# Conditioning in column groups, norm 1 by columns, attention among the gv and u chunks, and late dots that read PSUM

## The chip, the cores and the metric

One core of a Trainium2 chip runs the whole step as one program. The metric is the time of the program on the device in microseconds (us), lower is better. TensorE (PE) multiplies matrices; VectorE (DVE), ScalarE (ACT) and GpSimd (POOL) work on rows and tiles; SyncE (SP) issues most plain transfers. SBUF is the memory on the core, PSUM the eight banks (128 partitions of 512 f32 each) into which PE writes. All data is f32.

## The reference

One decoder layer for 512 prompt rows and 64 sample rows (8 sequences of 8, each with 256 cached keys), D = 1024. Cut to what matters:

```
mod = (silu(c) @ w_ada + b_ada)          # 1024 -> 6 x 1024, 9 conditions (1 prompt, 8 sample)
shift1, scale1, gate1, shift2, scale2, gate2 = mod
h = rmsnorm(x, g1) * (1 + scale1) + shift1
q, k, v, u, gv, gate_a, gate_b = split(h @ w_in)       # 7 x 1024 columns
gv = layernorm(gelu(gv), g_v, b_v); u = gelu(u)
out_b = stick_breaking_attention(q, k, v)              # 8 heads x 128
out_a = u * (causal 128x128 mix of gv rows)
x = x + gate1 * ((sigmoid(gate_a) * (out_a @ w_ba) + sigmoid(gate_b) * (out_b @ w_bb)) @ w_out)
h = rmsnorm(x, g2) * (1 + scale2) + shift2
for each of 8 heads: score 128 x 128 key pairs, keep the best 16 experts, softmax -> gates
x = x + gate2 * sum over the 128 experts of  gate * gelu(h . down[e]) * up[e]
y = rmsnorm(x, g_final)
```

Stick-breaking attention weights a key with exp(log sigmoid(z) + the sum of log sigmoid(-z) over the keys after it). Each of the 576 rows gathers 128 rows of `down` and 128 of `up`, 4 KB each, by its own expert numbers.

## The kernel before

**Tiles and groups.** The rows form five tiles of 128: prompt tiles 0 to 3 and SAMPLE, whose 64 rows stand twice in its tile. `GROUPS` is [[0], [1, 2], [3, SAMPLE]]. For each group a front runs: norm 1, q, k, v, attention, gv and u, the mix, the merge, the output projection, norm 2, the queries and the key scores. Then come the expert rows of its tiles, in the order 0, 1, 2, SAMPLE, 3.

**Events.** The expert work is written out by hand as events e = -16 ... 576, sixteen to a step of one head (two for SAMPLE), 36 steps. At event e POOL gathers `down` row e + 32 (L734, into a slot of `gather_ring` or another of eight late slots) and `up` row e + 16 (L749) with indirect DMAs in one fixed order; DVE makes the dot of a `down` row with `h2(t)` for 128 tokens at once (`dot`, L1665); ACT makes its gelu; and the `up` row is added, by `PE_SHARE` either on PE as a product with a diagonal of coefficients into banks 6 and 7 (`sum_row`, L1078) or on DVE (L1696). Every engine has its own copy of the event loop. A POOL gather waits until its slot has been used.

**Fronts.** Group 0's front runs ahead of all events on every engine. The fronts of groups 1 and 2 are generators cut into pieces, and `DUE`, from a cost list in `pieces`, says at which event each piece is taken up: group 1 from event -16 on, its first key scores asked for at event 90, its end at 126; group 2 from 128, asked at 346, its end at 380.

**Conditioning.** At the start SP loads the nine conditions, the first four chunks of `w_ada`, b_ada, both norm gains and the small constants, then x of all tiles, then the other 20 chunks. A chunk is 1024 rows x 256 columns, 1.05 MB, and there are four buffers (`NW`). ACT's Silu waits for five transfers. PE makes each chunk's nine rows with eight matmuls (L819), DVE adds b_ada to 256 columns of nine partitions, then makes (1 + scale) * gain. SP stores the result to DRAM twice (`mod_prompt`, and `mod_sample` with each row repeated eight times), waits, and only then goes on to q's chunks and to the row tables A1 = (1 + scale1) * g1 and B1 = shift1, which are read back broadcast over 128 partitions into the two buffers `row_tables`. Norm 1 on DVE multiplies x by 1/rms and A1 and adds B1; PE turns it in 128x128 blocks, and ACT copies the blocks into `hT`.

**Projections.** Weight chunks of 1024 x 256 go through the four buffers. `token_major` (L784, eight 128x256 matmuls) fills one PSUM bank per tile with 128 tokens x 256 columns, `channel_major` (L793) fills two banks with 128 channels each. Fills rotate over banks 0 to 3 with the semaphores `s_full` and `s_free`; transposes use banks 4 and 5. ACT copies q, k, v out and makes the gelu of gv and u (L1207, L1213); DVE and ACT empty the merge.

**Attention.** It goes by stages: in stage w PE makes the scores of the heads w + 1, the exponents (suffix sums) of the heads w and the outputs of the heads w - 1, two heads per stage in groups 0 and 1, one in group 2. ACT makes the log parts (abs, two relus, exp, ln: the table load of L1190 among them), then the Exp of the exponents, then copies the outputs. All stages of a group come first, then four gv chunks, then four u chunks, with the layer norm of gv on DVE beside the u chunks.

**Choices.** `choose` (DVE, top 16 keys of two halves, 256 pairs, top 16 again) is a generator of six parts, one to an event; `exponentials` on ACT and `weigh` on DVE give the gates. The choice of step m starts at event 16 (m - 2), that is a step before POOL needs its expert numbers.

Of the kernel before, what the change touches and what calls it, by code (L numbers as in the profile page):

```python
# [15 lines left out]
P = 128  # L16
# [19 lines left out]
WIDTH = 2 * P  # L36

# [13 lines left out]
CHOICES_OF = [[c for c, (m_, _, _) in enumerate(CHOICES) if m_ == m] for m in range(M)]  # L51

# [46 lines left out]

def pieces(g):  # L100

    T, heads = len(GROUPS[g]), head_groups(g)
    chunk = 7 if T == 2 else 6
    out = [("norm1", 6)] + [("project", chunk)] * 12
    out += [("attend", (8, 10, 7)[g])] * (len(heads) + 2)
    out += [("project", chunk)] * 8
# [7 lines left out]
def head_groups(g):  # L114

    items = [(i, t, hd) for i, t in enumerate(GROUPS[g]) if t != SAMPLE for hd in range(NH)]
    first = NH * sum(t != SAMPLE for ts in GROUPS[:g] for t in ts)
    items = [(first + w, *item) for w, item in enumerate(items)]
    size = 1 if g == LASTG else 2
    return [items[w:w + size] for w in range(0, len(items), size)]  # L120
# [24 lines left out]
def fill_base(g, phase):  # L145

    t = len(GROUPS[g])
    return NADA + group_base(g, 64, 16) + {"q": 0, "k": 8, "v": 8 + 4 * t, "gv": 8 + 8 * t, "u": 8 + 12 * t,
                                           "merge": 16 + 12 * t, "out": 48 + 12 * t, "query": 48 + 16 * t}[phase]
# [9 lines left out]
NCH = 48  # L159
# [3 lines left out]
def chunk_base(g, phase):  # L163

    pages = 2 * NDEC if g == LASTG else 0
    return NADA + NCH * g + {"q": 0, "k": 4, "v": 8, "gv": 12, "u": 16, "keys": 20, "values": 20 + NDEC,
                             "merge": 20 + pages, "out": 36 + pages, "query": 40 + pages}[phase]


def last_fill(n):  # L170

    if n < NADA:
        return n
    g = min((n - NADA) // NCH, LASTG)
    t = len(GROUPS[g])
    for phase, fills in (("query", 2), ("out", t), ("merge", 2), ("u", 2), ("gv", t), ("v", t), ("k", t), ("q", 2)):
        c = n - chunk_base(g, phase)
        if c >= 0:
            return fill_base(g, phase) + fills * (c + 1) - 1


def tables(g):

    kinds = ["p", "s"] if SAMPLE in GROUPS[g] else ["p"]
    return ([(w, k) for k in kinds for w in ("A1", "B1")] + [("gv", ""), ("bv", "")]
# [31 lines left out]

def build(nc, x_prompt, x_sample, cache_k, cache_v, page_table, c_prompt, c_sample, w_ada, b_ada,
# [1577 lines left out]
```

## Time and profile before

| | |
|---|---|
| time, median of 3 runs | 2562.68 us (2562.38 to 2566.64) |
| time of the profiled execution | 2551.76 us |
| span of the profiled execution | 2549.6 us, 24823 instructions |
| TensorE's mean granted clock | 0.874 of full speed |
| DMA | 849.21 MB, mean 333 GB/s; 604.05 MB of it gathers |

The profile is one execution. Its span runs from the first to the last instruction; its time and the median of the timed runs are a little larger. The page gives busy time by engine, then 40 slices of the span, then what each queue moved, the chain of work that ended last, and the costliest groups of instructions. A busy PE includes matmuls that run at a lower granted clock, and POOL's spans are rough.

### The profile page before, as it was taken

What the parts mean: (1) busy time and instruction counts of PE and PEld (TensorE: products, weight loads), DVE (VectorE), ACT (ScalarE), POOL (GpSimd) and SP (SyncE); (2) the same over time, 40 slices, a digit from 0 to 9 for tenths busy, and PEclk for the clock granted to TensorE, in tenths of its full rate; (3) what the DMA queues carried; (4) which work ended last, traced back from release to release, by engine and by line L of the source; (5) the groups of instructions that cost most, each with busy time, mean ns of one, the idle gap of its engine ahead of it and who ended that gap; (6) DMA issues with size and microseconds to landing.
All of it is one profiled execution on the core that took longest, in us unless ns stands there. A gap on an engine that the chain in (4) does not pass through costs nothing.

```text
span 2549.6 us, 24823 instructions
## 1 busy us (share of the span) xinstructions
PE 1925.6 (76%) x7928; PEld 1327.9 (52%) x7928; DVE 1565.4 (61%) x3434; ACT 535.6 (21%) x1168; POOL 1328.2 (52%) x1169
## 2 busy tenths in 40 slices
PE   6837986966899567588887789878676567667677
PEld 2336986855788444465565557656464222222222
DVE  0100115573987876776687867775779986667552
ACT  0004112164211112114522221111021112122121
POOL 0000002553555466565557656555467677777774
PEclk9968998988999788799997776888898799899999
DMA  8654787994899899899799979999999999999997
GB/s 273 202 174 151 274 281 253 344 349 168 336 379 413 338 394 373 303 412 359 263 375 405 409 282 402 377 367 367 347 370 330 347 361 369 357 382 388 371 381 297
DMA packets 218292, 849.21 MB, mean 333 GB/s; under 512 B 26383, under 2 KB 33807, under 8 KB 196586
## 3 DMA queue, kind: packets, MB, share of 16 engines
q0 software_dynamic: 165888, 604.05, 62.6%
q1 hardware_dynamic: 40148, 222.61, 23.6%
q10 hardware_dynamic: 12128, 20.98, 2.3%
q8 instruction: 64, 1.05, 0.2%
q14 instruction: 64, 0.52, 0.1%
HBM read 830.48 MB, written 16.80 MB: 332 GB/s over the span
## 4 chain that ended last, share of the span: by engine, by line
PE 39%; DMA 17%; POOL 12%; DVE 12%; issue 8%; ACT 6%; DVEq 3%; SPq 1%; ACTq 0%; POOLq 0%
PE bank L793 11%; PE bank L1078 9%; PE bank L784 9%; DMA gather_ring<-in_expert_down,expert_numbers 6%; DMA gather_ring<-in_expert_up,expert_numbers 5%; POOL gather_ring L749 5%; POOL gather_ring L734 5%; PE bank L819 3%; DVE expert_sums L1696 3%; DVE gather_ring L1665 2%; DMA v_tokens<-in_expert_up,expert_numbers 2%; POOL weight_chunks L734 2%; POOL v_tokens L749 1%; PE bank L1002 1%; DMA mod_sample<-gather_ring 1%
## 5 line engine op out<-in xcount | busy, mean ns | idle before, releaser
L734 POOL DMA_INDIRECT gather_ring<-in_expert_down,expert_numbers x488 | 584.8, 1198 | 876.5 <-DVEq L1632 400.1
L1078 PE MATMUL bank<-gather_ring,coef_diagonals 128*128 128x512 f32 x952 | 556.5, 729 | 317.9 <-ACT coef_diagonals L1323 168.0
L1665 DVE CUSTOM_DVE_ANT_0 gather_ring<-gather_ring,h_tiles 128x1024 f32<-128x1024 f32 x488 | 596.5, 1226 | 289.9 <-DMA gather_ring<-in_expert_down,expert_numbers 266.0
L749 POOL DMA_INDIRECT gather_ring<-in_expert_up,expert_numbers x510 | 569.0, 1116 | 271.7 <-issue 130.6
L1078 PEld LDWEIGHTS bank<-gather_ring,coef_diagonals 128*128 128x128 f32 x952 | 202.2, 227 | 607.2 <-issue 390.0
L793 PE MATMUL bank<-hT,weight_chunks 128*128 128x128 f32 (+2 forms) x2304 | 403.5, 336 | 7.0 <-issue 4.5
L793 PEld LDWEIGHTS bank<-hT,weight_chunks 128*128 128x128 f32 x2304 | 377.2, 199 | 51.8 <-issue 26.7
L1696 DVE SCALAR_TENSOR_TENSOR expert_sums<-gather_ring,expert_coefs,expert_sums 128x1024 f32<-128x1024 f32 x269 | 345.6, 1285 | 8.7 <-issue 8.7
L784 PE MATMUL bank<-weight_chunks,hT 128*128 128x256 f32 x960 | 211.7, 380 | 1.4 <-ACT qT L1207 1.4
L784 PEld LDWEIGHTS bank<-weight_chunks,hT 128*128 128x128 f32 x960 | 182.1, 191 | 31.5 <-issue 5.8
L1078 PE MATMUL bank<-v_tokens,coef_diagonals 128*128 128x512 f32 x264 | 130.5, 622 | 49.0 <-DMA v_tokens<-in_expert_up,expert_numbers 29.9
L1323 ACT ACTIVATE coef_diagonals<-identity,expert_coefs 128x128 f32<-128x128 f32 x304 | 108.1, 393 | 277.8 <-DVE expert_coefs L1676 117.4
L1665 DVE CUSTOM_DVE_ANT_0 weight_chunks<-weight_chunks,h_tiles 128x1024 f32<-128x1024 f32 x88 | 107.8, 1228 | 70.7 <-DMA weight_chunks<-in_expert_down,expert_numbers 67.6
L1078 PEld LDWEIGHTS bank<-v_tokens,coef_diagonals 128*128 128x128 f32 x264 | 46.6, 192 | 130.0 <-issue 87.6
L734 POOL DMA_INDIRECT weight_chunks<-in_expert_down,expert_numbers x88 | 95.1, 1081 | 26.8 <-issue 26.8
L819 PE MATMUL bank<-weight_chunks,condT 128*9 128x256 f32 x384 | 87.8, 393 | 3.0 <-DMA weight_chunks<-in_w_ada 2.7
L749 POOL DMA_INDIRECT v_tokens<-in_expert_up,expert_numbers x66 | 75.1, 1138 | 21.5 <-issue 14.0
L1379 ACT ACTIVATE expert_acts<-expert_dots 128x16 f32<-128x16 f32 x36 | 7.8, 216 | 372.3 <-DVEq L1668 372.2
L801 PE MATMUL bank<-identity,v_tokens 128*128 128x128 f32 x40 | 9.8, 427 | 86.0 <-DVE v_tokens L1465 71.6
L784 PE MATMUL bank<-weight_chunks,u_and_gv 128*128 128x256 f32 x320 | 70.5, 380 | 3.8 <-DVE u_and_gv L1532 3.7
L1430 DVE TENSOR_TENSOR gather_ring<-bank,gather_ring 9x256 f32<-9x256 f32 x24 | 9.9, 412 | 97.0 <-PE bank L819 97.0
L784 PEld LDWEIGHTS bank<-weight_chunks,u_and_gv 128*128 128x128 f32 x320 | 60.6, 190 | 15.1 <-issue 7.2
(217 smaller groups left out, 2112.1 us busy)
## 6 DMA issues: line engine op xcount, KB each, us to landing
weight_chunks<-in_w_in SPq DMA_DIRECT2D x84, 1024.0 KB
weight_chunks<-in_w_ada SPq DMA_DIRECT2D x24, 1024.0 KB
weight_chunks<-in_w_query SPq DMA_DIRECT2D x24, 1024.0 KB
weight_chunks<-in_w_branch_a SPq DMA_DIRECT2D x12, 1024.0 KB
weight_chunks<-in_w_branch_b SPq DMA_DIRECT2D x12, 1024.0 KB
weight_chunks<-in_w_out SPq DMA_DIRECT2D x12, 1024.0 KB
weight_chunks<-in_cache_k SPq DMA_DIRECT2D x16, 512.0 KB
weight_chunks<-in_cache_v SPq DMA_DIRECT2D x16, 512.0 KB
```

The costliest lines, as they stand in the source:

```text
L734: pool.indirect_dma_start(out=d_row(slot), out_offset=None, in_=down, in_offset=bass.IndirectOffsetOnAxis(ap=expert[:, t, h * TOPK + k:h * ...
L749: pool.indirect_dma_start(out=u_row(slot), out_offset=None, in_=up, in_offset=bass.IndirectOffsetOnAxis(ap=expert[:, t, h * TOPK + k:h * T ...
L784: mm = nc.tensor.matmul(out[:, 0:WC], src[:, k, :], w[:, k, :], start=(k == 0), stop=(k == KC - 1))
L793: mm = nc.tensor.matmul(out[:, 0:N], w[:, k, j * P:(j + 1) * P], src[:, k, 0:N], start=(k == 0), stop=(k == KC - 1))
L801: mm = nc.tensor.transpose(out[0:b.shape[1], j * P:j * P + b.shape[0]], b, ident[0:b.shape[0], 0:b.shape[0]])
L819: mm = nc.tensor.matmul(out[0:NG, 0:WC], cT[:, k, :], w[:, k, :], start=(k == 0), stop=(k == KC - 1))
L1002: mm = nc.tensor.matmul(bank[2][:, at], page_of(n, page)[:, hd * P:(hd + 1) * P], log_s[page][:, at], start=False, stop=(page == 1))
L1078: mm = nc.tensor.matmul(bank[6 + half], diag[:, n % 8, :], u_row(slot)[:, half * 512:(half + 1) * 512], start=(u == PE_TILE[t][0]), stop=( ...
L1323: nc.scalar.activation(diag[:, n % 8, :], ident[:], ACT.Copy, scale=coef[:, m % 2, k:k + 1]).then_inc(s_diag, 1)
L1430: nc.vector.tensor_tensor(m, read(n)[0:NG, 0:WC], m, ALU.add).then_inc(s_free[n % 4], 1)
L1665: nc.vector.tensor_tensor_reduce(out=row, in0=row, in1=h2(t), scale=1.0, scalar=0.0, op0=ALU.mult, op1=ALU.add, accum_out=dots[:, m % 2, k ...
L1696: nc.vector.scalar_tensor_tensor(out=a, in0=u_row(slot), scalar=by, in1=a, op0=ALU.mult, op1=ALU.add).then_inc(s_dsum, 1)
```

## The change

- **Conditioning.** `w_ada` is laid out by the host as 24 chunks of one modulation's 256 input rows x 1024 columns. `condition` runs four column groups: each of 256 columns writes nine partitions at partition 32q of bank 6 or 7. Eight chunks (shift1, scale1) come first; the other sixteen are put one each behind tile 0's q, k, v and gv chunks, in SP's list `CHUNKS` and on PE. DVE adds b_ada by quarters (`modulation`) and makes the gains (`with_gain`) in `modq`, 4 x 9 partitions.
- **First loads.** b_ada, the gains and the constants are issued on ACT's queue; Silu waits for the two transfers of conditions alone; x of tile 0 is the first load after them.
- **Norm 1.** PE turns scale and shift into columns (`modT`, 16 small transposes); DVE only multiplies x by 1/rms; ACT scales and shifts each 128x128 block as it copies it out of PSUM (Identity with scale and bias). For SAMPLE DVE does that with 16 small operations. The tables A1 and B1 are gone.
- **Stores.** `mod_prompt` and `mod_sample` are written in 36 DMAs on SP, after u's loads of group 0; SP waits for them before the G1 table and the merge weights.
- **gv and u among the attention stages** (`middle`): group 0 takes a gv or u chunk after each stage of two heads, group 1 goes by one head and takes one after every second stage, group 2 keeps attention first. ACT's order in a stage is now Exp, copy, log parts. Attention's buffers move to `h2_tiles` and `sigmoids`; the layer norm (`normalised`) follows at u's pieces.
- **Banks.** Fills rotate over two banks, 0 and 1; transposes use 2 and 3; attention's scores 4 and 5, its exponents bank 2 alone and its outputs bank 3 alone.
- **Times of the choices** (`CHOOSE`): tile 1's first choice is loaded at event 110, made in one go at event 111 and weighed at 117, the next at 115 to 127; the others stay. Group 1's key scores are asked for at event 106 instead of 90, its end is 127.
- **Late dots.** From step 26 (`X_FROM`) the dots read x from PSUM: ACT copies h2 of SAMPLE into banks 0 and 1 and of tile 3 into banks 4 and 5, at event 392.
- **Group 2** loads the A2 table before its first three query chunks; before it was after four.

The diff, cut:

```diff
+def middle(g):
+    attend = [("attend", w) for w in range(-1, len(head_groups(g)) + 1)]
+    fills = [(phase, c) for phase in ("gv", "u") for c in range(4)]
+    if g == LASTG:
+        return attend + fills
+    each = (1, 2)[g]
+    out = []
+    while attend or fills:
+        out += attend[:each] + fills[:1]
+        attend, fills = attend[each:], fills[1:]
+    return out
...
+AT_ONCE = CHOICES_OF[FIRST[1]][0]
+CHOOSE[AT_ONCE] = {"load": TOPK * 6 + 14, "start": TOPK * 6 + 15, "raise": TOPK * 7 + 3, "weigh": TOPK * 7 + 5}
+CHOOSE[AT_ONCE + 1] = {"load": TOPK * 7 + 3, "start": TOPK * 7 + 7, "raise": TOPK * 7 + 13, "weigh": TOPK * 7 + 15}
...
-    size = 1 if g == LASTG else 2
+    size = 2 if g == 0 else 1
...
-    for g, start, asked, heads, end in ((1, -TOPK, 90, 2, 126), (2, 8 * TOPK, 346, 3, 380)):
+    for g, start, asked, heads, end in ((1, -TOPK, 106, 2, 127), (2, 8 * TOPK, 346, 3, 380)):
...
+def chunks():
+    out = [("ada", 0, i) for i in range(8)]
...
+            if g == 0 and i < NADA - 8:
+                out.append(("ada", 0, 8 + i))
...
-            sp.dma_start(mod_p, mod9[0:1, :]).then_inc(s_modst, 16)
-            sp.dma_start(mod_s.rearrange("(b i) n -> b i n", i=DSEQ),
-                         mod9[1:NG, :].unsqueeze(1).broadcast_to([NDEC, DSEQ, NMOD * D])).then_inc(s_modst, 16)
-            sp.wait_ge(s_modst, 32)
...
+                    sp.wait_ge(s_modv, 4 * NMOD)
+                    sp.wait_ge(s_mod, 8)
...
+                    for q in range(4):
+                        sp.dma_start(rows[:, :, q], modq[32 * q:32 * q + 1]).then_inc(s_modst, 16)
+                        for i in range(DSEQ):
+                            sp.dma_start(by_token[:, i, :, q], modq[32 * q + 1:32 * q + NG]).then_inc(s_modst, 16)
+                    sp.wait_ge(s_modst, 16 * 4 * (DSEQ + 1))
...
-                if f >= 4:
-                    pe.wait_ge(s_free[f % 4], f // 4)
-                return bank[f % 4]
+                if f >= 2:
+                    pe.wait_ge(s_free[f % 2], f // 2)
+                return bank[f % 2]
...
+            def condition(i):
+                m, part = divmod(i, 4)
+                w = weight(NUMBER["ada", 0, i]).rearrange("p k n -> p (k n)")
+                if m >= 2 and part == 0:
+                    pe.wait_ge(s_modv, 4 * (m - 1))
+                for kk in range(2):
+                    for q in range(4):
+                        at = kk * D + q * QUARTER
+                        mm = nc.tensor.matmul(bank[6 + m % 2][32 * q:32 * q + NG, 0:QUARTER], cT[:, 2 * part + kk, :],
+                                              w[:, at:at + QUARTER], start=(part == 0 and kk == 0),
+                                              stop=(part == 3 and kk == 1))
+                mm.then_inc(s_ada, 1)
...
+                for q in range(4):
+                    rows = slice(32 * q, 32 * q + NG)
+                    nc.vector.tensor_tensor(modq[rows, m, :], bank[6 + m % 2][rows, 0:QUARTER], adaq[rows, m, :],
+                                            ALU.add).then_inc(s_modv, 1)
...
+                        for j in range(4):
+                            k = 4 * half + j
+                            ins = nc.scalar.activation(h[:, k, i * P:(i + 1) * P], src[:, j * P:(j + 1) * P], ACT.Identity,
+                                                       scale=modT[:, 1, k, 0:1], bias=modT[:, 0, k, 0:1])
...
-                    nc.vector.scalar_tensor_tensor(out=x, in0=x, scalar=r, in1=table(g, "A1", kinds[t]), op0=ALU.mult, op1=ALU.mult)
-                    dve.drain()
-                    nc.vector.tensor_tensor(x, x, table(g, "B1", kinds[t]), ALU.add).then_inc(s_n1h, 1)
+                    nc.vector.tensor_scalar(x, x, r, None, ALU.mult).then_inc(s_n1h, 1)
...
+                if e == TOPK * (X_FROM - 2) + 8:
+                    for row, at in ((h2(SAMPLE), 0), (h2(3), 4)):
+                        for half in range(2):
+                            nc.scalar.copy(bank[at + half], row[:, half * 512:(half + 1) * 512]).then_inc(s_xps, 1)
...
+                x = h2(t)
+                if m >= X_FROM:
+                    dve.wait_ge(s_xps, 4)
+                    x = banks[:, 0:D] if t == SAMPLE else banks[:, 4 * 512:4 * 512 + D]
+                nc.vector.tensor_tensor_reduce(out=row, in0=row, in1=x, scale=1.0, scalar=0.0, op0=ALU.mult,
...
+                    if c == AT_ONCE and e == at["start"]:
+                        for _ in choose(c):
+                            pass
+                    elif c and c != AT_ONCE and 0 <= e - at["start"] < 6:
```

## Rows read from the trace of the kernel before

**Rows 1.** The page: busy time by engine, and GB/s in 40 slices.

```profile
PE 1925.6 (76%) x7928; PEld 1327.9 (52%) x7928; DVE 1565.4 (61%) x3434; ACT 535.6 (21%) x1168; POOL 1328.2 (52%) x1169
...
GB/s 273 202 174 151 274 281 253 344 349 168 336 379 413 338 394 373 303 412 359 263 375 405 409 282 402 377 367 367 347 370 330 347 361 369 357 382 388 371 381 297
```

**Rows 2.** The chain in order of time: start, us, what.

```profile
115.82 32.57 DMA mod_sample<-gather_ring
...
150.67 11.94 DMA row_tables<-mod_prompt
```

**Rows 3.** Windows to 343: length, then PE, PEld, DVE, ACT, POOL, PEclk, DMA, GB/s.

```profile
2.00:13.00 11.00, 0.00 (x0) 0.00 (x0) 0.06 (x1) 0.09 (x1) 3.12 (x10) 1.00 0.97 382
...
113.00:168.00 55.00, 4.92 (x24) 3.44 (x22) 8.94 (x14) 3.19 (x6) 0.00 (x0) 0.53 0.43 124
168.00:213.00 45.00, 44.59 (x264) 40.74 (x264) 0.00 (x0) 6.20 (x20) 0.00 (x0) 0.96 0.56 199
213.00:250.00 37.00, 20.13 (x96) 18.07 (x96) 0.00 (x0) 25.51 (x66) 0.00 (x0) 0.72 0.41 157
250.00:283.00 33.00, 30.29 (x209) 28.47 (x210) 8.96 (x13) 9.34 (x18) 0.00 (x0) 1.00 0.61 229
283.00:343.00 60.00, 58.91 (x512) 58.72 (x512) 7.01 (x24) 5.73 (x17) 0.00 (x0) 0.97 0.82 295
```

**Rows 4.** Timeline of the first 30 us: start, us, engine, line, what.

```profile
1.55 2.12 SPq L521 DMA_DIRECT2D weight_chunks<-in_w_ada  x4
...
19.52 1.06 ACT L1111 ACTIVATE gather_ring<-gather_ring 9x1024 f32<-9x1024 f32 x1 [17.43 <-DMA expert_sums<-in_g_norm]
```

**Rows 5.** Groups by form: count, busy us, mean ns of one, idle before.

```profile
L784 PE MATMUL bank<-weight_chunks,hT 128*128 128x256 f32 x960 | 211.7, 380 | 1.4 <-ACT qT L1207 1.4
...
L819 PE MATMUL bank<-weight_chunks,condT 128*9 128x256 f32 x384 | 87.8, 393 | 3.0 <-DMA weight_chunks<-in_w_ada 2.7 <-issue 0.3
...
L1190 ACT ACT_TABLE_LOAD x20 | 25.7, 1283 | 1.0
...
L1213 ACT ACTIVATE u_and_gv<-bank 128x256 f32<-128x256 f32 x20 | 7.7, 384 | 64.6 <-PE bank L784 64.6
```

**Rows 6.** Windows from 425 us on, columns as in rows 3.

```profile
425.00:513.00 88.00, 87.28 (x402) 76.11 (x400) 54.18 (x124) 16.25 (x41) 44.97 (x38) 0.97 0.87 321
513.00:634.00 121.00, 79.54 (x385) 62.50 (x384) 63.29 (x109) 68.54 (x136) 58.30 (x47) 0.86 0.72 264
634.00:703.00 69.00, 57.30 (x272) 50.50 (x272) 63.10 (x120) 16.14 (x29) 38.65 (x32) 0.93 0.85 321
703.00:862.00 159.00, 142.61 (x656) 124.84 (x656) 128.77 (x260) 17.64 (x30) 87.72 (x71) 0.96 1.00 393
862.00:962.00 100.00, 63.88 (x247) 47.42 (x248) 76.61 (x139) 16.19 (x39) 61.41 (x54) 0.78 0.95 363
...
2052.00:2500.00 448.00, 316.94 (x625) 118.53 (x624) 290.75 (x745) 82.60 (x208) 352.07 (x315) 0.94 0.99 375
```

**Rows 7.** DVE's timeline near 634; in brackets the idle before and its end.

```profile
634.07 0.49 DVE L1576 MAX8 top_values<-key_scores 128x8 f32<-128x128 f32 x2 [38.03 <-DMA key_scores<-key_scores]
```

**Rows 8.** Timelines of POOL and DVE near 2008 and 2253.

```profile
2007.19 1.22 DVE L1711 TENSOR_TENSOR expert_sums<-bank,expert_sums 128x1024 f32<-128x1024 f32 x1
...
2008.06 0.94 POOL L749 DMA_INDIRECT gather_ring<-in_expert_up,expert_numbers  x1 [0.30 <-issue]
...
2253.01 1.22 DVE L1665 CUSTOM_DVE_ANT_0 gather_ring<-gather_ring,h_tiles 128x1024 f32<-128x1024 f32 x1
...
2253.37 1.68 POOL L749 DMA_INDIRECT v_tokens<-in_expert_up,expert_numbers  x1 [0.30 <-issue]
```

**Rows 9.** A late window (columns as in rows 3), and one of POOL's waits in 2100:2460.

```profile
2220.00:2260.00 40.00, 30.45 (x58) 12.23 (x59) 28.85 (x73) 11.75 (x29) 32.02 (x27) 0.88 1.03 408
...
POOL gather_ring L749 <- PE bank L1078: 7.0, 23, 0.3
```

More of the change, by code:

```diff
@@ L96, with head_groups @@
 U_AT = places(lambda u: u % U_EARLY if u // TOPK < LATE else u % U_LATE)
+def head_groups(g):
+    items = [(i, t, hd) for i, t in enumerate(GROUPS[g]) if t != SAMPLE for hd in range(NH)]
+    first = NH * sum(t != SAMPLE for ts in GROUPS[:g] for t in ts)
+    items = [(first + w, *item) for w, item in enumerate(items)]
+    size = 2 if g == 0 else 1
+    return [items[w:w + size] for w in range(0, len(items), size)]
+def middle(g):
[9 more added lines that the diff above has]
+    return out
 def pieces(g):
-    T, heads = len(GROUPS[g]), head_groups(g)
+    T = len(GROUPS[g])
     chunk = 7 if T == 2 else 6
     out = [("norm1", 6)] + [("project", chunk)] * 12
-    out += [("attend", (8, 10, 7)[g])] * (len(heads) + 2)
-    out += [("project", chunk)] * 8
+    out += [(what, (7, 5, 7)[g] if what == "attend" else chunk) for what, _ in middle(g)]
     if g == LASTG:
@@ L526, in load_table, with load_through @@
+            def load_through(phase, g, c):
+                last = NUMBER[phase, g, c]
+                while loaded[0] < len(CHUNKS) and (loaded[0] <= last or CHUNKS[loaded[0]][0] == "ada"):
+                    load_chunk(loaded[0])
+                    loaded[0] += 1
             def load_table(g, what, kind):
@@ L663, in _ @@
                     load_table(g, "B2", "s")
[L664 to L668 removed]
+                load_through("query", g, NH - 1)
             sp.wait_ge(s_kst, 16 * TILES)
@@ L814, in _ @@
             pe.wait_ge(s_tfree[1], 1)
-            for n in range(NADA):
-                w = weight(n)
-                out = take(n)
-                for k in range(KC):
-                    mm = nc.tensor.matmul(out[0:NG, 0:WC], cT[:, k, :], w[:, k, :], start=(k == 0), stop=(k == KC - 1))
-                mm.then_inc(s_full[n % 4], 1)
+            def condition(i):
[10 more added lines that the diff above has]
+                mm.then_inc(s_ada, 1)
+            for i in range(8):
+                condition(i)
             pe.wait_ge(s_small, 16 * NSMALL)
@@ L955, in page_scores @@
                             at = hd * NS + b * DSEQ
-                            mm = nc.tensor.matmul(bank[2 + page][:, at:at + DSEQ],
+                            mm = nc.tensor.matmul(bank[4 + page][:, at:at + DSEQ],
                                                   turned_page[m_ % 2][:, hd * P:(hd + 1) * P],
@@ L981, in front @@
                         rows = NS if part == 2 else P
-                        out = bank[(4, 5, 1)[part]][0:rows, :]
+                        out = bank[(2, 3, 1)[part]][0:rows, :]
                         nc.tensor.matmul(out, since[0:rows, 0:rows], log_s[part], start=True, stop=False)
@@ L1490, in front @@
+                for what, c in middle(g):
+                    if what == "u":
+                        normalised(c)
+                    elif what == "gv" and c == 3 and g == 0:
+                        modulation(5)
+                        dve.wait_ge(s_g2, 16 * 4)
+                        with_gain(4, 1)
                     yield
```

564 lines of the change are left out of this document (302 added, 262 removed).

## The prediction

> **What bounds the kernel now.** I read the page first, then the chain of waits, then busy time by stage, then single stages. The page says that no engine fills the span: PE 76%, DVE 61%, POOL 52%; the DMA rate runs from 151 GB/s early to about 410 [rows 1]. So the stages differ, and there are three.
>
> Until 404 us only tile 0's front runs, and no expert row moves. The chain [rows 2] goes through the conditioning, a 33 us store of `mod_sample` and a 12 us table load, before norm 1 can end. From 113 to 168 us PE is busy 4.9, DVE 8.9 and ACT 3.2 us of 55, and DMA runs at 124 GB/s [rows 3]. Then come 45 us of q, k, v at PE's pace, 37 us of attention in which PE is busy 20 and DMA moves 157 GB/s, 33 us of gv, u and the mix, and 121 us from the first merge chunk on.
>
> From 407 to 962 us tile 0's 128 rows run beside group 1's front. Over these windows [rows 6] DMA moves 181 MB, and 703:862 shows that 393 GB/s is possible. The dip is attention, 513:634, at 264 GB/s: PE is busy 80 of 121, ACT 69. DVE stood 38 us there, waiting for key scores [rows 7]: ACT asks for them in order, and ACT was behind in attention.
>
> From 2052 to 2500 us both fronts are over. POOL issues 315 gathers in 448 us, 1.42 us each, and is busy 352 us [rows 6]. Between two issues it idles 0.3 us and waits for hardly anyone [rows 9]: POOL is the bound, with DMA close behind (0.99 busy, 375 GB/s).
>
> **The front of tile 0.** Removed from the start of the path: 16 of 24 conditioning chunks, the mod store, the A1 and B1 tables.
>
> Conditioning: the first 11 us moved 382 GB/s [rows 3], 2.75 us a chunk of 1.05 MB. Eight chunks, tile 0's x and some 1.5 MB of constants are 10.5 MB, 28 us: landed at 30. Silu began at 19.5 behind a 17.4 us wait for norm gains [rows 4]; it now waits for the two condition rows alone, so DMA decides. If the four column groups run together, PE keeps up; if they take turns, a chunk costs PE what it costs today, 87.8/24 = 3.66 us [rows 5], and eight end near 38.
>
> Between the last chunk and the first q chunk lie sums, gain, spatial transposes, norm 1 and its turn. These were the busy times of 113:168 [rows 3], together 17 us; the new small transposes and per-column scaling add a few, the two dropped table passes, and sixteen of the 24 adds that now come later, take as many away. So q starts at 47 (55 if they take turns), not 168.
>
> q, k, v and twelve conditioning chunks: 24 chunks, 4 already landed. At 350 GB/s (between 382 and the 295 that PE's pace allowed around 300 us) a chunk is 3.0 us: 60, plus 3 for k and v stores, 3.5 for the last chunk: 66 instead of 45, to 113. Taking turns, PE decides: 45 + 12 x 3.66 = 89, to 144.
>
> Attention with gv and u between: attention's 37 us is a chain through ACT and stays. Four stages now carry a gelu, one more table load (1.28 us [rows 5]) and single banks for exponents and outputs: 2.5 us each, 10 together. gv and one u chunk vanish in the gaps; three u chunks (3.5 us each by the 256-column row, 211.7/60 [rows 5]) and 4 us of mix stay: 62 instead of 70, to 175. The layer norm moves beside the u chunks.
>
> The mod store now stands on SP between u's loads and the merge weights, in 36 DMAs. Four SP issues took 2.12 us [rows 4], so 36 take 19; with 3 us for DVE and 6 for landing, from the last conditioning chunk near 158, SP is free at 186 and the first merge chunk lands at 192. What was a stall ahead of norm 1 is now a smaller one ahead of the merge: 17 us. Were the stores as slow as the one of before (33 us), it would be 27; were they hidden, 0.
>
> From there 121 us as before: 313, that is **-91** against 404. Both ends: taking turns 348 (-56); 380 GB/s and no store stall 288 (-116).
>
> **Tile 0's rows beside group 1.** 513:703 takes 190 us [rows 6] for sixteen heads, then eight gv and u chunks and two layer norms. PE's busy time in it is 137. One head per stage with a chunk after every second one lets chunk matmuls run while ACT does logs; ACT gets 8 more table loads, 10 us. A head's own chain (exponents on PE, exp, logs, copy) keeps it above PE's 137; I take 160, **-30**. Norm 1's two table passes go, but eight scaled activations replace two copies: nothing, hidden by DVE's and PE's other work.
>
> The first key scores are asked for at event 106 instead of 90. This gives the front sixteen more events to spread over and so should remove more of the standing of DVE: another -30. The price: the first choice for tile 1 is made at one go at event 111, and POOL, in order, can't issue the gather of row 128 until it ends, nor the up rows queued behind it; DVE and PE then wait for their landing. Six steps of about 1.5 us and a landing of 6 to 8: +15. Sum **-45**. Ends: 181 MB at 393 GB/s is 461 us of 555, at best -80 beside some stall; at worst +10, when only the choice's stall comes.
>
> **Events in the middle (962 to 2052).** Norm 1 for the sample tile loses its table loads; the last group's A2 table now stands on SP ahead of three query chunks and waits for the out phase. Both are about 10 us and cancel. Two fill banks in place of four cost nothing where the copy out (0.38 us [rows 5]) hides beside the other bank's fill (3.5); without that cover see the rivals. 0, +-20.
>
> **Late dots.** A gather takes POOL 0.94 us or more: one that began 0.36 us into a dot took 1.68 and ended 0.8 us after the dot did; yet one that began during a 128x1024 add which reads `bank` took 0.94 [rows 8]. So two SBUF inputs hold POOL up, one PSUM input doesn't. The Trainium skill (SBUF — State Buffer, Who interferes with whom) says the first half, and adds an inference that a two-input tensor operation leaves descriptor generation alone; by that inference these dots would gain nothing, and the rows say otherwise.
>
> With x in PSUM for steps 26 to 35 POOL could issue every 0.94 + 0.30 = 1.24 us, which is 421 GB/s. A 40 us stretch of gathers alone reached 408 [rows 9]. I take 400, 1.31 us each: 315 x (1.42 - 1.31) = **-35**. Ends: 0 if DMA at 0.99 busy is the bound already, -55 at POOL's pace. The add from `bank` took 1.22 us like the dot [rows 8], so DVE pays nothing. Four copies into PSUM on ACT hide: it is busy 83 of 448 us.
>
> **Sum.** -91 - 45 - 35 = -171. The profiled execution took 2551.8 us (span 2549.6), the median 2562.7, 11 above: 2551.8 - 171 + 11 = **2392 us**. A change of less than 0.2% is what a measurement of this kernel can't tell from none.
>
> **Rivals.** (1) The column groups take turns: nothing in this trace runs matmuls on part of the columns side by side. For: all of today's matmul rows follow one another. Against: four different output quadrants. Front -56 instead of -91: 2427. The Trainium skill (TensorE: Matmul & The Clock Gate, Part 3: Packing small matmuls) gives 2.38 times for three column tiles; no run here shows it, and by it a chunk is an estimated 1.5 us and the sum as forecast.
>
> (2) DMA is the late bound: a gather-only stage with DMA 0.99 busy may not go above 375 GB/s. Against it the 408 above. Late dots 0: 2427. The Trainium skill (DMA: Bandwidth & Descriptors, Where 436 GB/s comes from) puts HBM's limit for a core at about 358 GB/s, which would make this case certain; 375 over 448 us and 408 over 40 are above it.
>
> (3) Tile 0's rows give nothing back, because the at-once choice and single banks cost what the gaps gain: 2437.
>
> (4) Slower: two fill banks. Groups 1 and 2 have 96 fills each. If PE, before a fill, waits for an ACT or DVE that stands at another event (in a dot, in a table load), the 171 us are gone at 171/192 = 0.9 us a fill: from there this decides. At one dot a fill (1.22 us [rows 8]) it is 234 us, and 2392 + 234 = 2626. For: DVE empties the branch fills between its dots. Against: in the gelu rows ACT stood 65 us waiting for PE, not PE for ACT [rows 5].
>
> (5) It shows no difference: the front's gain is given back in waits of the same sum, 0.9 us a fill in (4): 2563.
>
> **How the numbers follow.** Forecast 0.55; (1) 0.17; (2) 0.12; (3) 0.08; (4) 0.06; (5) 0.02. The first four are faster: 0.92; same 0.02; slower 0.06. Range: the bounds of the front (-116 to -56) and of rows and dots (-135 to +10) taken to about two thirds each way give 2330 to 2460; cases (1) to (3) lie in it, (4) outside.
>
> **What would show it.** First q chunk near 47 and first dot near 316. `mod_sample` stores on SP between u and merge, with PE idle under 20 us. No DVE wait of 38 us for key scores, but one POOL wait at the choice for tile 1. From step 26 on POOL's gathers near 0.94 us and a DMA rate near 400. I am wrong if q starts after 60, if PE's waits for evacuations in groups 1 and 2 add up to over 50 us, or if gathers shorten and the late rate stays at 375.

## The result and the profile after

The changed kernel takes 2494.57 us (median of four runs, 2490.67 to 2500.41), the kernel before 2564.66 (2562.38 to 2568.31): a ratio of 0.9727, interval 0.9704 to 0.9751. It is faster by 70 us where 171 were forecast, and outside the range of 2330 to 2460. One execution of `e1_logs_first_g2` further down ran at a lower granted clock, 0.77 instead of 0.87, and took 2546.53 us; it is left out of that kernel's numbers.

The first dot of a step in DVE's timeline marks where each stretch ends. Both columns are profiled executions (2551.76 and 2490.67 us; the first lies 10.6 us under the fastest of that kernel's four timed runs):

| stretch | before | after | difference | forecast |
|---|---|---|---|---|
| front of tile 0, to the first dot | 407.6 | 333.2 | -74.4 | -91 |
| steps 0 to 7 (tile 0's rows, group 1's front) | 554.9 | 525.7 | -29.2 | -45 |
| steps 8 to 25 (group 2's front beside rows) | 1090.0 | 1160.0 | +70.0 | 0 |
| steps 26 to the end (late dots) | 497.1 | 469.6 | -27.5 | -35 |
| span | 2549.6 | 2488.5 | -61.1 | -171 |

Three of the four go the way of the forecast and fall 17, 16 and 7.5 us short of it. The third, where nothing was forecast, gives back more than half of what the others won, and of its 70 us, 40.5 stand in steps 11 and 12 (129.2 before, 169.7 after), 10.4 in step 22 (69.1, 79.5) and 13.2 in steps 17 to 19 (188.0, 201.2); the remaining 5.9 are spread.

The page after, GB/s in 40 slices, answers to [rows 1]:

```profile
GB/s 271 346 242 241 265 270 376 399 298 341 389 411 359 252 396 284 407 304 168 285 359 378 352 320 371 338 365 365 348 322 343 337 390 395 393 409 408 409 409 269
```

The late slices rose to 409. The nineteenth is the lowest, 168: it lies in step 12. The front's windows after, columns as in [rows 3], and three pieces of the chain in order of time (start, us, what) as in [rows 2]:

```profile
13.00:35.00 22.00, 11.66 (x128) 3.72 (x128) 1.70 (x5) 0.28 (x2) 0.00 (x0) 0.80 1.04 378
35.00:54.40 19.40, 7.12 (x43) 5.55 (x43) 8.35 (x19) 5.38 (x16) 0.00 (x0) 0.50 0.73 258
54.40:124.00 69.60, 61.84 (x456) 47.57 (x456) 3.37 (x8) 6.20 (x20) 0.00 (x0) 0.93 0.81 310
124.00:190.40 66.40, 52.02 (x372) 44.25 (x368) 11.90 (x22) 40.21 (x86) 0.00 (x0) 0.92 0.65 230
190.40:209.90 19.50, 0.01 (x1) 0.00 (x0) 2.09 (x4) 0.00 (x0) 0.00 (x0) 0.58 0.47 138
209.90:270.00 60.10, 59.37 (x512) 59.20 (x512) 6.93 (x24) 5.73 (x17) 0.00 (x0) 0.97 0.87 312
270.00:333.20 63.20, 51.27 (x360) 48.60 (x360) 16.79 (x56) 11.11 (x31) 3.92 (x4) 0.92 0.79 271
```

```profile
34.92 6.36 issue
...
199.00 3.85 DMA mod_sample<-gather_ring
203.29 6.40 DMA weight_chunks<-in_w_in
```

The rows give the parts of the forecast one by one: the first q chunk at 54.4 (forecast 47), q, k, v and twelve conditioning chunks 69.6 us (66), attention with gv, u and the mix 66.4 (62), PE idle for the stores 19.5 (17), from the merge on 123.3 (121).

Two lines of PE's timeline (start, us, engine, line, what) tell whether the column groups run together:

```profile
60.27 0.81 PE L822 MATMUL bank<-hT,weight_chunks 128*128 128x128 f32 x5
61.01 1.05 PE L855 MATMUL bank<-weight_chunks,condT 128*9 128x256 f32 x16
```

A conditioning chunk is eight matmuls of 256 columns in both kernels, sixteen records here. They pass in 1.05 us, where eight that followed one another took 3.66 [rows 5]. The groups don't take turns.

Steps 11 and 12 are group 2's attention. These are windows of the two steps, first of the kernel before, then of the changed kernel (PE, PEld, DVE, ACT, POOL, PEclk, DMA share, GB/s):

```profile
1149.00:1213.00 64.00, 51.26 (x205) 34.05 (x204) 40.48 (x84) 31.41 (x49) 36.87 (x33) 0.92 0.92 359
1213.00:1278.00 65.00, 57.04 (x231) 37.51 (x230) 40.87 (x85) 34.05 (x55) 38.60 (x33) 0.97 0.75 266
```

```profile
1048.00:1120.00 72.00, 51.95 (x184) 34.63 (x183) 41.54 (x85) 24.39 (x38) 31.17 (x32) 0.86 0.83 314
1120.00:1218.00 98.00, 70.89 (x252) 44.70 (x251) 40.16 (x84) 39.78 (x64) 36.41 (x33) 0.83 0.51 177
```

DVE's and ACT's work is the same to within 1.3 us, and POOL's is 8 us less. PE makes 436 matmul records in both, but in 122.8 instead of 108.3 us, at a lower granted clock. The rest of the 40 us is waiting. ACT's waits over the two steps say for what (us in total, times, longest), first before, then after:

```profile
ACT u_and_gv L1180 <- PE bank L877: 24.8, 8, 4.7
...
ACT u_and_gv L1203 <- PE bank L893: 8.4, 1, 8.4
```

```profile
ACT u_and_gv L1287 <- PE bank L955: 73.6, 8, 9.8
...
ACT u_and_gv L1265 <- PE bank L939: 3.4, 1, 3.4
```

Before, ACT waited for scores (L877), 3 us a stage, and only once for exponents (L893). After, it waits for exponents (L955) in each of the eight stages, 9.2 us a time. One stage of the changed kernel in ACT's timeline:

```profile
1137.61 0.60 ACT L1287 ACTIVATE u_and_gv<-bank 128x512 f32<-128x512 f32 x1 [9.84 <-PE bank L955]
1138.51 0.27 ACT L1291 COPY qT<-bank 128x128 f32<-128x128 f32 x1 [0.29 <-PE bank L965]
1138.67 0.69 ACT L1265 ACTIVATE u_and_gv<-bank,stick_bias 128x512 f32<-128x512 f32 x1
...
1142.52 0.63 ACT L1275 ACTIVATE u_and_gv<-u_and_gv 128x512 f32<-128x512 f32 x1
...
1144.59 0.39 ACT L1416 ACTIVATE coef_diagonals<-identity,expert_coefs 128x128 f32<-128x128 f32 x1
```

ACT stands 9.84 us until PE's exponents are done, then makes Exp, the copy and the log parts of the next head (these from 1138.67 to 1143.15), and PE can't begin that head's exponents before they are there. What ACT does for the rows (L1416, the diagonals) stands behind the wait too; PE's sums wait for the diagonals, and POOL for the sums, as its timeline shows for the same stage:

```profile
1149.08 1.71 POOL L778 DMA_INDIRECT gather_ring<-in_expert_up,expert_numbers  x1 [13.85 <-PE bank L1138]
```

A second cost comes with the wait. In the same stage PE stood 5.03 us for the diagonals, and the products after it (the rows' sums, then scores) ran at a granted clock of 0.50 (1.2 GHz); before, PE had stood 0.87 us and the same products ran at 1.00 (2.4 GHz). PE's timeline and a window around these products, first before, then after:

```profile
1199.65 1.98 PE L1078 MATMUL bank<-gather_ring,coef_diagonals 128*128 128x512 f32 x4 [0.87 <-ACT coef_diagonals L1323]
...
1199.65:1202.52 2.87, 2.87 (x14) 1.91 (x15) 1.53 (x3) 0.00 (x0) 2.26 (x3) 1.00 1.03 408
```

```profile
1126.53 3.78 PE L1138 MATMUL bank<-gather_ring,coef_diagonals 128*128 128x512 f32 x4 [5.03 <-ACT coef_diagonals L1416]
...
1126.53:1132.02 5.49, 5.49 (x14) 3.42 (x14) 2.85 (x12) 1.24 (x1) 1.14 (x2) 0.50 0.00 1
```

The same 14 records take 5.49 instead of 2.87 us.

### The profile page after: what moved, and what is told of

Read it like the earlier page. It is cut to its first block, busy times and chain, and to the rows that moved or that the text cites. A ratio compares the mean times of both kernels' runs of the same rounds, so it can differ in the third digit from the quotient of the medians.

```text
span 2488.5 us, 25049 instructions
## 1 busy us (share of the span) xinstructions
PE 1888.3 (76%) x7944; PEld 1316.6 (53%) x7944; DVE 1558.6 (63%) x3451; ACT 572.2 (23%) x1217; POOL 1265.7 (51%) x1169
## 3 DMA queue, kind: packets, MB, share of 16 engines
q8 instruction: 64, 1.05, 0.2%
## 4 chain that ended last, share of the span: by engine, by line
PE 39%; DMA 20%; DVE 15%; POOL 8%; issue 8%; ACT 5%; DVEq 5%; SPq 1%; ACTq 1%; POOLq 0%
PE bank L822 12%; PE bank L1138 9%; PE bank L813 8%; DMA gather_ring<-in_expert_down,expert_numbers 8%; DMA gather_ring<-in_expert_up,expert_numbers 4%; DVE expert_sums L1831 4%; POOL gather_ring L778 3%; POOL gather_ring L763 3%; DVE gather_ring L1800 2%; DMA weight_chunks<-in_w_in 2%; DMA v_tokens<-in_expert_up,expert_numbers 1%; POOL weight_chunks L763 1%; DMA key_scores<-key_scores 1%; PE bank L1062 1%; SPq L671 1%
## 5 line engine op out<-in xcount | busy, mean ns | idle before, releaser
L763 POOL DMA_INDIRECT gather_ring<-in_expert_down,expert_numbers x488 | 569.3, 1167 | 797.7 <-DVEq L1763 357.9
L1138 PE MATMUL bank<-gather_ring,coef_diagonals 128*128 128x512 f32 x952 | 566.1, 740 | 327.9 <-ACT coef_diagonals L1416 191.1
L778 POOL DMA_INDIRECT gather_ring<-in_expert_up,expert_numbers x510 | 545.6, 1070 | 346.7 <-PE bank L1138 198.0
L1800 DVE CUSTOM_DVE_ANT_0 gather_ring<-gather_ring,h_tiles 128x1024 f32<-128x1024 f32 x408 | 498.3, 1226 | 234.8 <-DMA gather_ring<-in_expert_down,expert_numbers 213.2
L822 PE MATMUL bank<-hT,weight_chunks 128*128 128x128 f32 (+2 forms) x2304 | 408.3, 339 | 32.6 <-DMA weight_chunks<-in_w_in 19.5
L822 PEld LDWEIGHTS bank<-hT,weight_chunks 128*128 128x128 f32 x2304 | 380.5, 202 | 80.8 <-issue 59.6
L813 PE MATMUL bank<-weight_chunks,hT 128*128 128x256 f32 x960 | 219.9, 389 | 20.7 <-DMA weight_chunks<-in_w_in 20.7
L1416 ACT ACTIVATE coef_diagonals<-identity,expert_coefs 128x128 f32<-128x128 f32 x304 | 108.7, 393 | 285.1 <-DVE expert_coefs L1811 126.2
L1800 DVE CUSTOM_DVE_ANT_0 gather_ring<-gather_ring,bank 128x1024 f32<-128x1024 f32 x80 | 97.7, 1221 | 61.0 <-DMA gather_ring<-in_expert_down,expert_numbers 55.3
L1800 DVE CUSTOM_DVE_ANT_0 weight_chunks<-weight_chunks,bank 128x1024 f32<-128x1024 f32 x80 | 97.0, 1220 | 55.2 <-DMA weight_chunks<-in_expert_down,expert_numbers 51.5
L763 POOL DMA_INDIRECT weight_chunks<-in_expert_down,expert_numbers x88 | 84.9, 965 | 26.9 <-issue 22.6
L778 POOL DMA_INDIRECT v_tokens<-in_expert_up,expert_numbers x66 | 61.9, 937 | 26.6 <-issue 16.8
L822 PE MATMUL bank<-u_and_gv,weight_chunks 128*128 128x128 f32 (+2 forms) x384 | 66.4, 333 | 3.7 <-ACT sigmoids L1361 3.7
```

The source lines that it names most:

```text
L763: pool.indirect_dma_start(out=d_row(slot), out_offset=None, in_=down, in_offset=bass.IndirectOffsetOnAxis(ap=expert[:, t, h * TOPK + k:h * ...
L778: pool.indirect_dma_start(out=u_row(slot), out_offset=None, in_=up, in_offset=bass.IndirectOffsetOnAxis(ap=expert[:, t, h * TOPK + k:h * T ...
L813: mm = nc.tensor.matmul(out[:, 0:WC], src[:, k, :], w[:, k, :], start=(k == 0), stop=(k == KC - 1))
L822: mm = nc.tensor.matmul(out[:, 0:N], w[:, k, j * P:(j + 1) * P], src[:, k, 0:N], start=(k == 0), stop=(k == KC - 1))
L1138: mm = nc.tensor.matmul(bank[6 + half], diag[:, n % 8, :], u_row(slot)[:, half * 512:(half + 1) * 512], start=(u == PE_TILE[t][0]), stop=( ...
L1416: nc.scalar.activation(diag[:, n % 8, :], ident[:], ACT.Copy, scale=coef[:, m % 2, k:k + 1]).then_inc(s_diag, 1)
```

## The experiments

Each kernel ran beside the kernel before on one chip; times are medians, ratios are to the kernel before.

### ACT's order in group 2

```diff
                     if what == "attend":
+                        if g == LASTG and c + 1 < len(groups):
+                            log_parts(groups[c + 1])
                         for n, i, t, hd in groups[c] if 0 <= c < len(groups) else []:
...
-                        if c + 1 < len(groups):
+                        if g != LASTG and c + 1 < len(groups):
                             log_parts(groups[c + 1])
```

> The changed kernel with one edit: in group 2 alone ACT makes the log parts of the next head first in a stage, as the kernel before did, then Exp and copy. Theory A (ACT's new order puts log parts of head w+1 behind Exp of head w, so PE's exponents and ACT's log parts no longer run side by side): the eight stages, 16.7 us apart in the changed kernel and 10.3 before, come back to about 11, steps 11 and 12 lose some 40 us, the time is about 2455 (2440 to 2470). Rival B (the single banks for exponents and outputs make the stage long): spacing stays near 16 us and the time at 2494 (2485 to 2500).

Measured: 2445.01 us (2444.11 to 2452.0), ratio 0.9563 (0.951 to 0.9617), against 0.9727 of the changed kernel. Steps 11 and 12 take 63.0 and 64.3 us. Its windows of the two steps:

```profile
1043.00:1106.00 63.00, 50.27 (x204) 33.86 (x203) 40.70 (x85) 31.23 (x48) 34.62 (x32) 0.95 0.95 366
1106.00:1170.00 64.00, 56.13 (x234) 36.75 (x233) 40.46 (x85) 34.21 (x55) 35.46 (x32) 0.97 0.74 262
```

Theory A holds, B falls: with single banks for exponents and outputs still in place, the two steps are as long as before the change, and PE's granted clock is back at 0.95 and 0.97. The other way round, on the kernel before:

```diff
-                    if w + 1 < len(groups):
+                    if g != LASTG and w + 1 < len(groups):
                         log_parts(groups[w + 1])
...
+                    if g == LASTG and w + 1 < len(groups):
+                        log_parts(groups[w + 1])
```

> The kernel before with one edit: in group 2 alone ACT makes Exp and copy of a stage ahead of the log parts of the next head, as the changed kernel does; exponents and outputs keep two banks each. Theory A (the order alone is the loss): stages go from 10.3 to 16 or 17 us, steps 11 and 12 grow by 40 to 48 us together, the time is 2563 + 44 = 2607 (2595 to 2615). Rival B (order and single banks are needed together for the loss): 2563 to 2580.

Measured: 2609.45 us (2600.72 to 2621.54), ratio 1.0165 (1.0116 to 1.0214), +42.7 us. The windows of the two steps show the changed kernel's 72 and 98 us and its 177 GB/s:

```profile
1140.00:1212.00 72.00, 52.22 (x182) 34.12 (x182) 41.10 (x86) 24.40 (x38) 33.91 (x32) 0.83 0.83 314
1212.00:1310.00 98.00, 70.76 (x249) 44.23 (x249) 40.19 (x84) 39.91 (x64) 36.36 (x34) 0.83 0.51 177
```

The order alone makes the loss, from either kernel.

### The same order in group 1, and the chunks among its stages

With log parts first in groups 1 and 2 (the edit above with `g` in place of `g == LASTG`):

> The changed kernel with ACT's old order in groups 1 and 2. Group 1 has a gv or u chunk after every second stage. Theory A: these chunks cover the wait, so group 1's order costs little: 2448 (2442 to 2454), steps 1 to 4 within 5 us. Rival B: group 1's sixteen stages pay it too, 2 to 3 us each: 2448 - 40 = 2408 (2400 to 2425).

Measured: 2451.25 us (2441.78 to 2461.12), ratio 0.9552 (0.9508 to 0.9596): no change against log parts first in group 2 alone. Theory A for the time. (Steps 1 to 4 take 267.3 us against 257.9 with log parts first in group 2 alone, more than the 5 us allowed, and longer where B said shorter.) Then, with log parts first in group 2 alone, group 1's chunks were put behind its attention:

```diff
-    if g == LASTG:
+    if g >= 1:
         return attend + fills
```

> The changed kernel with ACT's old order in group 2 and group 1's gv and u chunks after all its attention stages, still one head per stage and asked for at event 106. Theory A (the chunks between the stages are what made tile 0's rows shorter): DMA falls again in attention, steps 1 to 4 lose 20 to 30 us, the time is about 2470 (2462 to 2480). Rival B (the later asking point and norm 1 made them shorter, or DMA sets their pace): 2448 (2442 to 2456).

Measured: 2493.96 us (2490.29 to 2500.5), ratio 0.9738 (0.9701 to 0.9774): 45 us lost by the ratios, more than A said. Steps 3 and 4 take 96.4 and 82.2 us (68.8 and 62.4 with the chunks). That could be the chunks' own worth, or the new order left without cover; so log parts first in group 1 as well:

> As the kernel with group 1's attention first, and in group 1 too ACT makes the log parts first in a stage (its old order), so both groups 1 and 2 have that order. It asks where the 45 us went that group 1 lost without chunks among its stages. Theory A (the new order without cover, the same loss as in group 2): the sixteen stages run side by side again, steps 3 and 4 come back near 68 and 62 us, the time is 2452 (2444 to 2462). Rival B (the chunks among the stages are worth it themselves, since ACT alone is busy in attention and the gelus then wait together): 2485 to 2500.

Measured: 2449.51 us (2441.81 to 2455.68), ratio 0.9564 (0.9539 to 0.9589). Theory A: it all comes back. (Steps 3 and 4 take 59.6 and 80.1 us, other than expected: the chunks now stand together in step 4.) Windows of group 1's attention, from the Exp in its first log parts to its last Exp of exponents, first with attention first and the new order, then with the old order:

```profile
437.80:577.40 139.60, 91.76 (x366) 71.69 (x366) 81.73 (x162) 89.30 (x145) 67.91 (x55) 0.77 0.73 267
```

```profile
434.80:530.50 95.70, 69.37 (x366) 57.35 (x366) 78.22 (x159) 90.15 (x147) 60.98 (x50) 0.93 0.95 357
```

The same attention takes 95.7 instead of 139.6 us and moves 357 instead of 267 GB/s; here too PE makes the same 366 records, at a granted clock of 0.93 instead of 0.77. The chunks among the stages and the new order belong together: the chunks give PE work while ACT makes log parts, and cover in group 1 what the order costs. With the old order there is nothing to cover, and the chunks gain nothing that these runs can tell.

### Dots from SBUF

```diff
-X_FROM = 26
+X_FROM = M + 4
```

> The changed kernel with all dots reading x from SBUF, and without the four copies into PSUM. Theory A: PSUM's x frees POOL; steps 26 to 35 go back from 42 us to 44 to 46 us a step, gathers from 0.96 to 1.13 us, the time is longer by 25: 2520 (2510 to 2530). Rival B (DMA bounds the late steps, and they got shorter for another reason, such as banks or phase): steps stay near 42 to 43 us, 2495 (2488 to 2502).

Measured: 2518.47 us (2509.43 to 2521.93), ratio 0.9825 (0.9779 to 0.987), +24 us against the changed kernel. One of POOL's four groups over steps 27 to 34 (count, busy us, mean ns) and the window of the same stretch, first of the changed kernel, then with all dots from SBUF:

```profile
L778 POOL DMA_INDIRECT gather_ring<-in_expert_up,expert_numbers x83 | 78.5, 946 | 39.5 <-PE bank L1138 22.7 <-issue 16.8
...
2063.90:2408.20 344.30, 257.55 (x513) 97.76 (x512) 235.49 (x601) 69.03 (x170) 249.28 (x264) 0.94 1.03 405
```

```profile
L778 POOL DMA_INDIRECT gather_ring<-in_expert_up,expert_numbers x81 | 98.3, 1213 | 24.7 <-issue 21.0 <-PE bank L1138 3.7
...
2062.00:2440.00 378.00, 262.20 (x516) 97.40 (x514) 238.73 (x605) 69.05 (x170) 299.55 (x258) 0.94 0.98 364
```

Theory A. DVE's busy time is nearly equal (235 and 239 us). POOL's gathers change, over all four groups from 1.16 us (299.55 us for 258) to 0.94 (249.28 for 264), and the rate with them, from 364 to 405 GB/s. The stretch from step 26 on parts the two in every profile here: 469 to 471 us in the nine with late dots from PSUM, 494 to 505 in the four with dots from SBUF.

### The choices of tile 1

The old times for tile 1's choices (`AT_ONCE` and its two entries of `CHOOSE` left out) and 90 and 126 in `due()`:

> The changed kernel with the old times of tile 1's choices: key scores asked for at event 90, group 1's end at 126, no choice made at one go. Theory A, as forecast: the later point gains 30 us and the choice at one go costs 15, so this is slower by about 15: 2510. Rival B: the choice at one go costs more than the later point gains (POOL stood 27 us there, step 7 took 90 us): 2480 (2465 to 2487). In both cases POOL has no wait of 27 us in step 7, and DVE waits again for the first key scores, by A some 38 us, by B under 20 because attention among gv and u no longer holds ACT up.

Measured: 2494.17 us (2490.2 to 2497.79), ratio 0.9742 (0.97 to 0.9784): no difference to the changed kernel, and a time between those of the two theories. The wait of POOL is real. The changed kernel's POOL in step 7:

```profile
854.33 0.93 POOL L763 DMA_INDIRECT gather_ring<-in_expert_down,expert_numbers  x1 [27.05 <-DVEq L1763]
```

It is gone with the old times, and step 7 takes 51.5 instead of 90.4 us; but steps 1, 2 and 6 are longer by 16.5, 9.3 and 11.8; group 1's front has sixteen events less there. Steps 0 to 7 take 537.6 us against 525.7 of the changed kernel, and by the first dot of step 26, at 2020.6 against 2018.9, little of that is left. DVE's wait for the first key scores was 4.5 us in this run, not 38: it went without the later asking point.

### The stores of the modulation

```diff
                     for q in range(4):
+                        load_through("merge", g, 3 * q + 2)
                         sp.dma_start(rows[:, :, q], modq[32 * q:32 * q + 1]).then_inc(s_modst, 16)
```

> The changed kernel with the 36 stores of the modulation put on SP in four parts behind the loads of merge chunks 2, 5, 8 and 11 of group 0, instead of all ahead of them. Theory A: the 19.5 us in which PE stands ahead of the merge is on the path, so the first dot comes at 317 instead of 333 and the time falls by 15: 2479 (2470 to 2486). Rival B: the start is won and given back in the steps beside group 1's front: first dot at 317, time at 2494 (2488 to 2500).

Measured: 2482.97 us (2474.91 to 2495.46), ratio 0.9687 (0.9643 to 0.9732): -11.6 us, though the intervals overlap. The median is in Theory A's range; the profiled execution, 2495.46 us, is the slowest of the four, and there the start is given back by the first dot of step 26 (2024.1 against 2018.9), as B says. The first dot comes at 320.8 instead of 333.2. In SP's queue of the changed kernel eight of the 36 stores take this long (start, us):

```profile
169.44 6.82 SPq L671 DMA_DIRECT2D mod_sample<-gather_ring  x8
```

All 36 go from 168.6 to 200.3. They are the cause of the wait ahead of the merge; spread, they give back 12.4 of its 19.5 us.

### Two fill banks

In the kernel before, every rotation of fills over four banks became one over two:

```diff
-                if f >= 4:
-                    pe.wait_ge(s_free[f % 4], f // 4)
-                return bank[f % 4]
+                if f >= 2:
+                    pe.wait_ge(s_free[f % 2], f // 2)
+                return bank[f % 2]
```

> The kernel before with its fills rotating over banks 0 and 1 alone, nothing else changed. In the changed kernel with ACT's old order the steps 14 and 16 to 19, beside group 2's u, mix and merge, still take 19 us more than before. Theory A (two banks are why: PE waits in the merge for DVE's or ACT's emptying): these steps grow by 15 to 25 us, group 1's merge in steps 4 to 6 by as much or less, the time is 2585 to 2610. Rival B (two banks cost nothing, as forecast, since a copy hides beside the other bank's fill): 2557 to 2569.

Measured: 2567.8 us (ten runs), ratio 1.0 (0.9973 to 1.0027). Theory B: two banks cost nothing in this kernel. Its profile has 1110.4 us in steps 8 to 25, where the shown profile of the kernel before has 1090.0, with equal medians. Steps 17 to 19 take 188.0 us in that profile, 198.6 here, 205.6 in the kernel before with log parts last, which has four banks, and 193.9 to 205.2 in the ten profiles of the changed kernel and its variants. The shown profile of before is low there, so the 13 us of these steps can't be told from the spread between executions.

### Group 2's tables

```diff
+                if SAMPLE in tiles:
+                    load_through("query", g, NW - 1)
                 load_table(g, "A2", "p")
-                load_through("query", g, NW - 2)
+                if SAMPLE not in tiles:
+                    load_through("query", g, NW - 2)
                 load_table(g, "B2", "p")
```

> The changed kernel with ACT's old order in group 2 and, for that group, the tables A2 and B2 loaded behind four query chunks as before (changed: A2 ahead of three, B2 behind them). Theory A: step 22, 79.9 us against 69.1 before, is longer because B2 stands behind query chunks that cannot land until the out phase has used their buffers, and DVE waits 8 us more in norm 2; so step 22 returns to about 70 and the time to 2448 - 10 = 2438 (2432 to 2443). Rival B: the longer step is norm 2 meeting other work, 2448 (2443 to 2455).

Measured: 2441.45 us (2429.28 to 2446.24), ratio 0.9498 (0.9457 to 0.9539), against 0.9563 without the edit; the intervals overlap, and the medians are 4 us apart. The trace is plainer: step 22 takes 69.8 instead of 79.9 us. DVE's waits in it, in the changed kernel and then with the edit:

```profile
DVE h_tiles L1696 <- DMA row_tables<-mod_prompt: 8.4, 1, 8.4
DVE h_tiles L1694 <- DMA row_tables<-mod_sample: 6.9, 1, 6.9
```

```profile
DVE h_tiles L1699 <- DMA row_tables<-mod_sample: 5.9, 1, 5.9
```

The wait of 8.4 us for B2 (`mod_prompt`) is gone. Theory A for the step; for the time the runs only lean that way.

### The three edits together

> The changed kernel with the three edits that helped together: ACT's old order in group 2, that group's A2 and B2 behind four query chunks, and the modulation's stores spread behind merge chunks of group 0. Theory A (three separate places, so they add): first dot near 320, step 22 near 70, 2448 - 7 - 11 = 2430 (2420 to 2440). Rival B (an earlier start is given back beside the fronts): 2441 (2437 to 2450).

Measured: 2427.72 us (six runs, 2420.81 to 2440.12), ratio 0.9487 (0.9456 to 0.9518). First dot at 319.4, steps 11, 12 and 22 at 62.3, 66.1 and 70.9 us. By its median Theory A (they add), though the interval doesn't part it from the kernel without spread stores. It beats both kernels: 136 us under the kernel before, 67 under the changed one.

## Why the prediction was wrong, point by point

**The step that failed is "Events in the middle: 0, +-20".** It priced norm 1's tables, A2 and the banks there, and put ACT's order in a stage at nothing, although the change moves `log_parts` in all groups and group 2 has no chunks among its stages. I took attention for "a chain through ACT" that stays. It was not one chain: in group 2 PE made the exponents of head w while ACT made the log parts of head w + 1. The new order puts them in series: Exp of the exponents starts every 16.6 us instead of every 10.2, rows on ACT, PE and POOL queue up behind each wait, and PE, which stands longer, is granted a lower clock. That is +42.7 us on the kernel before; taken away from the changed kernel, 42 us by the ratios and 46.6 by the spans (2488.5 and 2441.9). Without it the changed kernel takes 2445 us, inside the range.

The same step had a smaller miss. A2 and norm 1's tables were said to cancel; B2's place behind query chunks costs 10 us in step 22, and nothing was seen to pay for it. Of the remaining 19 us 13 are in steps 17 to 19, where executions differ by as much.

**Front of tile 0, -91: right in kind, -74.** The column groups run together, the store stall (17) came as 19.5. Mis-sized was q's start, 47 against 54.4: the conditioning ended at 34.9 instead of 30, and 6.4 us passed before PE could turn the spatial weights, whose small loads the change puts on ACT's queue, which I had costed at nothing (that these loads are what PE waited for was not tried). Attention took 4 us more, q to v 4, the stores and what follows 5; the first dot of before came at 407.6 and not at the 404 from which -91 was taken.

**Tile 0's rows, -45: -29, and for another reason.** The choice at one go made POOL stand 27 us, where 15 were priced, and with the later asking point it is worth nothing in time; the two were not tried apart. The 30 us for chunks among the stages are not there either; they cover the new order. DVE's wait of 38 us [rows 7] did go, in the run with the old times too (4.5 us there). What made these steps 29 us shorter (one head a stage, norm 1 by columns, or when group 1's front falls) stays open; no run parted them, and that -29 came near -45 is luck.

**Late dots, -35: -27.5, and right.** From 2018.9 to 2440 us POOL issued 321 gathers, 1.31 us each, as was said. The Trainium skill (SBUF — State Buffer, Who interferes with whom) infers that `tensor_tensor`, with two inputs, leaves descriptor generation alone; the dots from SBUF, with two inputs as well, differ from it, 1.16 us a gather against 0.94. The shortfall is at the end: over the last 80 us POOL, now ahead, waits 17.5 us for PE's sums, where it waited 6.1 us before.

**Rivals.** (1) is out by 1.05 us a chunk. (2) is out by 405 GB/s over 344 us. The Trainium skill (DMA: Bandwidth & Descriptors, Where 436 GB/s comes from) puts HBM's limit for a core near 358; here, with one core at work, the measurement goes above it. DMA is now at 1.03 busy, so by that share this stretch has little left. (3) is out by the 29 us of tile 0's rows, (5) by the ratio. (4), two fill banks, is out by a ratio of 1.0 on the kernel before, and in the changed kernel by PE's waits for ACT and DVE ahead of fills, 16.1 us in all from 333 to 2019. Of the other side's mechanisms I had the wrong one: the loss came from the order on an engine, not from banks.

**Range and signs.** None of the three signs of being wrong came: q started at 54.4, the waits ahead of fills add up to 16.1 us, and the late rate rose. All three watched steps that had a price. The range's rule, two thirds of the way from -171 to the bounds' sum of -46, gives 2475 as its upper end and not 2460; the result lies outside that as well.

## What to carry to other kernels

Where an engine's instructions change places in a loop, write down for one round which engine works while which other waits, before and after, and do so for every variant of the loop: an order that is covered by inserted work in one group is bare in the group that has none. An interleaving and an order that come as a pair are each to be tried alone; here the pair was worth nothing over neither. And a wait on an engine that also serves a second stream of work costs that stream as well; here it cost PE part of its clock too.

## What the runs showed of the hardware

Four column groups of nine partitions ran a chunk in 1.05 us instead of 3.66, 3.5 times as fast for the same product. The granted clock was 1.00 (2.4 GHz) there and 0.98 over the chunks of the kernel before (42 to 112 us), as windows show; this one is of the changed kernel, around one such chunk (columns as in [rows 3]):

```profile
61.00:62.10 1.10, 1.10 (x18) 0.45 (x17) 0.00 (x0) 0.27 (x1) 0.00 (x0) 1.00 0.19 22
```

The Trainium skill (TensorE: Matmul & The Clock Gate, Part 3: Packing small matmuls) has 2.38 times for three column tiles, from which 1.5 us was estimated; the trace shows more, with four.

The stores of eight partitions cost SP some 0.85 us each in the issue (6.82 us for eight), against 0.53 for a weight chunk of 1.05 MB [rows 4]. A gather's issue on POOL shows what DVE reads: 1.16 us beside dots with two inputs in SBUF, 0.94 beside dots with one in PSUM, with DVE busy 239 and 235 us. And in group 2's attention the products after 5 us in which PE stood ran at a granted clock of 0.50, 14 records in 5.49 us, and after 0.87 us at 1.00, in 2.87.
